# A two-layer decoder on one Trainium2 core: the order of loads, row sums and norms at the start and at the two layer ends

## The reference, cut to what matters

```python
for layer in range(2):
    hn = rmsnorm(h, attn_norm[layer])
    h = h + (even_mixer, odd_mixer)[layer](hn, ...)    # two kinds of attention each, then a projection
    h = h + hierarchical_moe(rmsnorm(h, ffn_norm[layer]), ...)
return rmsnorm(h, final_norm)
```

## Time and profile before

| | |
|---|---|
| median of 3 executions | 1095.43 us (1093.26 to 1098.76) |
| the profiled execution | 1096.88 us, span 1095.0 us |
| mean granted TensorE clock | 0.986 of full |
| PE busy | 1001.8 us (91%) |
| DVE, ACT, POOL busy | 386.8, 233.9, 91.6 us |
| moved by DMA | 276.95 MB, mean 253 GB/s |

### The profile page before, as it was taken

One profiled execution on the slowest core, in us unless ns is written; L12 is line 12 of the kernel. 1 busy time (PEld: TensorE's weight loads), 2 busy tenths in 40 slices (PEclk: granted clock), 3 DMA queues, 4 the chain that ended last, 5 costly groups with the idle time before them and its releaser, 6 DMA issues.

```text
span 1095.0 us, 12899 instructions
## 1 busy us (share of the span) xinstructions
PE 1001.8 (91%) x5140; PEld 575.4 (53%) x5140; DVE 386.8 (35%) x1103; ACT 233.9 (21%) x605; POOL 91.6 (8%) x103
## 2 busy tenths in 40 slices
PE   5999999999998999999788998899999999998866
PEld 3344644455455656666434647536455666665532
DVE  3123621336145323222243316547225333222215
ACT  3122620236011000000022216537202100000002
POOL 2000000000101011211101001000100111111100
PEclk9999999999999999999999999999999999999998
DMA  9522205964336999999999420023624899999996
GB/s 330 215 91 76 77 2 174 210 266 168 120 125 228 407 420 419 420 419 419 421 348 334 165 77 1 11 77 154 237 96 168 325 420 419 421 418 420 416 374 226
DMA packets 63549, 276.95 MB, mean 253 GB/s; under 512 B 12787, under 2 KB 17379, under 8 KB 38906
## 3 DMA queue, kind: packets, MB, share of 16 engines
q1 hardware_dynamic: 53088, 256.95, 60.9%
q0 software_dynamic: 10400, 19.16, 5.0%
HBM read 261.94 MB, written 30.44 MB: 267 GB/s over the span
## 4 chain that ended last, share of the span: by engine, by line
PE 66%; DMA 20%; DVE 5%; SPq 3%; issue 2%; ACT 2%; POOL 1%; POOLq 0%; DVEq 0%; ACTq 0%
PE bank L841 13%; PE bank L931 10%; PE bank L1054 9%; PE bank L853 9%; DMA K<-rows,small 7%; PE bank L872 5%; PE bank L1068 5%; DMA D<-in_moe_w_down 5%; DMA hnT<-in_moe_w_down 3%; PE bank L883 3%; DMA W<-in_moe_w_up 2%; PE bank L899 2%; SPq L449 2%; PE bank L1241 2%; DMA oT<-in_o_w_in 1%
## 5 line engine op out<-in xcount | busy, mean ns | idle before, releaser
L841 PE MATMUL bank<-hnT,W 128*128 128x512 f32 x336 | 145.1, 593 | 0.8 <-ACT hnT L1334 0.8
L1068 PE MATMUL bank<-D,PT 128*64 128x512 f32 x416 | 105.1, 611 | 10.1 <-DMA D<-in_moe_w_down 7.4
L841 PEld LDWEIGHTS bank<-hnT,W 128*128 128x128 f32 x336 | 63.5, 190 | 80.5 <-issue 79.5
L1054 PE MATMUL bank<-W,PT 128*64 128x256 f32 x640 | 78.6, 386 | 13.0 <-DMA W<-in_moe_w_up 6.7
L1759 DVE SCALAR_TENSOR_TENSOR PT<-bank,small,PT 128x256 f32<-128x256 f32 x32 | 15.5, 484 | 210.8 <-PE bank L1054 210.8
L1781 DVE SCALAR_TENSOR_TENSOR K<-K,small,bank 128x512 f32<-128x512 f32 x64 | 47.8, 747 | 86.7 <-PE bank L1068 86.5
L1054 PE MATMUL bank<-W,cst 128*64 128x256 f32 x640 | 77.5, 381 | 0.0
L872 PE MATMUL bank<-K,Q 128*128 128x256 f32 (+3 forms) x256 | 70.4, 417 | 6.1 <-ACT K L1353 3.4
L853 PE MATMUL bank<-W,hnT 128*128 128x512 f32 (+2 forms) x256 | 71.4, 439 | 0.0
L1368 ACT ACTIVATE P<-P,nm 128x256 f32<-128x256 f32 (+3 forms) x128 | 68.3, 535 | 14.6 <-DVE nm L1551 14.1
L1408 ACT ACTIVATE PT<-bank 128x256 f32<-128x256 f32 x32 | 12.3, 384 | 271.9 <-PE bank L1060 271.9
(11 more groups left out here) (245 smaller groups left out, 1364.1 us busy)
## 6 DMA issues: line engine op xcount, KB each, us to landing
D<-in_moe_w_down SPq DMA_DIRECT2D x48, 1024.0 KB, 22.8
W<-in_moe_w_gate SPq DMA_DIRECT2D x40, 1024.0 KB
W<-in_moe_w_up SPq DMA_DIRECT2D x40, 1024.0 KB, 19.6
hnT<-in_moe_w_down SPq DMA_DIRECT2D x12, 1024.0 KB, 17.7
W<-in_e_w_in SPq DMA_DIRECT2D x5, 2048.0 KB
expert_rows<-K SPq DMA_DIRECT2D x2, 4096.0 KB, 34.8
V<-in_moe_w_gate SPq DMA_DIRECT2D x6, 1024.0 KB
Q<-in_moe_w_gate SPq DMA_DIRECT2D x6, 1024.0 KB
```

The source lines that it names most:

```text
L841: last = nc.tensor.matmul(b[:, :], w[:, k, 128 * fb:128 * fb + 128], hnT[:, k, :], start=(k == 0), stop=(k == KD - 1))
L1054: last = nc.tensor.matmul(bank[b][at, 0:256], XT[k // 4][:, k % 4, at], w[:, 256 * k:256 * k + 256], start=(k == 0), stop=(k == KD - 1))
L1068: last = nc.tensor.matmul(bank[5 + half][at, :], hT[:, 128 * c + 64 * a:128 * c + 64 * a + 64], d[:, col:col + 512], start=(c == 0), stop= ...
```

## The change

It has five parts.

1. Start: `gain` for the first norm is loaded by SP as the second transfer, ahead of `cst`, on a semaphore of its own; POOL's load and SP's wait for it go. The transposes of odd chunks use banks 1 and 2, and DVE and ACT copy later in their order.
2. The up weights of experts 30 and 31 come in four half loads, the first halves of both on `s_ulast`; PE waits for each half by itself.
3. Layer 0: the oT weights are issued ahead of all rows, before SP's wait for the scatters.
4. DVE runs `add_row(0)` ahead of `finish(lay, 15)`, and norms chunk 0 (layer 0) before `add_row(1)`. In layer 0, PE transposes chunk 0 after all four late products.
5. Layer 1: PE adds `y_in` by the identity for chunk 3 only (before: chunks 1 and 2); DVE adds chunks 1 and 2.

```diff
-        summed = [(), (1, 2)]
+        first_bank = (3, 1)
+        summed = [(), (3,)]
...
             for c in range(C):
                 sp.dma_start(h[:, c, :], x[0, 128 * c:128 * c + 128, :]).then_inc(s_x[c], 16)
                 if c == 0:
+                    sp.dma_start(gain, attn_norm[0:1, :].partition_broadcast(128).rearrange("a b n -> a (b n)"))\
+                      .then_inc(s_gain0, 16)
                     sp.dma_start(cst[:, 0:C_MASKS], const_table[:, 0:C_MASKS]).then_inc(s_const, 16)
...
-                    load_half(lay, 2 * p, 1)
-                    load_half(lay, 2 * p + 1, 1)
+                    if p < NP - 1:
+                        load_half(lay, 2 * p, 1)
+                        load_half(lay, 2 * p + 1, 1)
+                    else:
+                        for part in range(2):
+                            for e in (2 * p, 2 * p + 1):
+                                up = expert_slot(lay, e)[0][1]
+                                half = slice(DM * part, DM * part + DM)
+                                sp.dma_start(up[:, half], wu_v[lay][e][:, half])\
+                                  .then_inc((s_ulast, ups_landed(lay, p)[0])[part], 16)
...
-            sp.wait_ge(s_gain, 16)
...
             def load_expert_rows(lay):
+                if lay == 0:
+                    sp.wait_ge(s_gu, 11)
+                    load_cols("oT", odd_tile[0], owin_v, 0, 512)
                 for i in range(NB):
                     sp.wait_ge(s_sc[i], 16 * SCATTERS[i] * (lay + 1))
...
                 for c in range(C):
-                    if lay == 0 and c == 3:
-                        load_cols("oT", odd_tile[0], owin_v, 0, 512)
...
-            load_gain(0)
...
-                    if c:
-                        pe.wait_ge((s_ntA, s_ntV)[half], c)
+                    if c >= 2:
+                        pe.wait_ge((s_ntA, s_ntV)[half], c - 1)
...
-                    pe.wait_ge(*ups_landed(lay, p))
-                    product(3, [slot[0][1] for slot in pair], lambda half: None).then_inc(s_gu, 1)
+                    landings = [ups_landed(lay, p)] * 2
+                    if p == NP - 1:
+                        landings[0] = s_ulast, 32 * (lay + 1)
+                    product(3, [slot[0][1] for slot in pair], lambda half: pe.wait_ge(*landings[half])).then_inc(s_gu, 1)
...
-                    if c == 3 and lay == 0:
-                        transpose_second(0)
...
+            transpose_second(0)
             latent_rows(0)
...
                 add_row(0)
+                finish(lay, NP - 1)
                 add_late(0)
                 if lay == 0:
+                    norm_chunk(2, 0)
                     add_row(1)
-                    norm_chunk(2, 0)
                     add_late(1)
...
                 else:
+                    add_row(1)
+                    add_late(1)
                     norm_chunk(4, 0)
-                    add_late(1)
-                    add_row(3)
+                    add_row(2)
+                    add_late(2)
                     norm_chunk(4, 1)
-                    add_late(2)
                     add_late(3)
...
             for c in range(C):
                 norm_chunk(0, c)
-                if c:
-                    norm_out(c - 1)
+                if c >= 2:
+                    norm_out(c - 2)
+            norm_out(C - 2)
             norm_out(C - 1)
...
-            finish(0, NP - 1)
...
-            finish(1, NP - 1)
```

More of the change, by code:

```diff
@@ L324, in trunk @@
         s_dlast = sem("last_down_halves_loaded")
+        s_ulast = sem("last_ups_first_halves_loaded")
         s_half = sem("half_of_first_tile_loaded")
         s_gain = sem("gain_loaded")
+        s_gain0 = sem("first_gain_loaded")
         s_sq = sem("squares_summed")
@@ L805, in transpose_normed @@
                 for half in range(2):
-                    if c:
-                        pe.wait_ge((s_ntA, s_ntV)[half], c)
+                    if c >= 2:
+                        pe.wait_ge((s_ntA, s_ntV)[half], c - 1)
                     for kk in range(4):
                         k = 4 * half + kk
-                        last = nc.tensor.transpose(bank[3 + half][:, 128 * kk:128 * kk + 128],
+                        last = nc.tensor.transpose(bank[first_bank[c % 2] + half][:, 128 * kk:128 * kk + 128],
                                                    hn_row[:, c, 128 * k:128 * k + 128], ident)
@@ L1303, in norm @@
                     mean_root(v, c)
-                    if v == 0 and c >= 2:
-                        norm_out(c - 2)
+                    if v == 0 and c == 2:
+                        norm_out(0)
                     if v == 2 and c == 0:
@@ L1311, in norm @@
                 if v == 0:
-                    norm_out(2)
-                    norm_out(3)
+                    for c in range(1, C):
+                        norm_out(c)
                 if v == 2:
@@ L1334, in norm_out @@
                 nc.scalar.activation(hnT[:, 0:4, 128 * c:128 * c + 128],
-                                     bank[3][:, :].rearrange("p (k t) -> p k t", k=4), ACT.Copy).then_inc(s_ntA, 1)
+                                     bank[first_bank[c % 2]][:, :].rearrange("p (k t) -> p k t", k=4), ACT.Copy)\
+                  .then_inc(s_ntA, 1)
             def norm_out_second(c):
@@ L1510, in norm_chunk @@
                 if c == 0:
-                    dve.wait_ge(s_gain, 16 * (v // 2 + 1))
+                    dve.wait_ge(*((s_gain, 16 * (v // 2)) if v else (s_gain0, 16)))
                 nc.vector.scalar_tensor_tensor(hn_row[:, c, :], h[:, c, :], rstd[:, c:c + 1], gain,
@@ L1517, in norm_out @@
                 nc.vector.tensor_copy(hnT[:, 4:8, 128 * c:128 * c + 128],
-                                      bank[4][:, :].rearrange("p (k t) -> p k t", k=4)).then_inc(s_ntV, 1)
+                                      bank[first_bank[c % 2] + 1][:, :].rearrange("p (k t) -> p k t", k=4)).then_inc(s_ntV, 1)
             def norm_out_second(c):
```

## The result

The changed kernel takes 1104.83 us, the median of five executions (1101.74 to 1105.68). Five executions of the kernel before have the median 1097.33. The ratio is 1.0066, 95% interval [1.0053, 1.0079], so it is slower by some 7.2 us. Forecast were 3.2 us more, and the time is above the end of the range (1102.5). The profiled execution took 1104.83 us with a span of 1102.9 us and a mean granted clock of 0.987. DMA moves the same 276.95 MB, and PE is busy for 997.2 us where it was for 1001.8, so what the kernel is longer by is waiting of PE.

A forecast was written before the change was run, and what follows sets the result against it. PE was taken as the bound, DMA-saturated expert stretches moving with it. Start -1.3, layer 0 +3.2, layer 1 +1.1 and half loads +0.2 gave +3.2 on 1095.4, so 1098.6 us; 8-in-10 range 1091.0 to 1102.5.

The forecast's parts named there:

- R: End of layer 0: landing time of chunk 0's rows, 564.5 before the change, taken as 568.8 after it.
- the term of layer 0: End of layer 0: later end of the first latent product, R - 565.6 = +3.2 us, bounds +1.0 and +4.3.
- even sharing: End of layer 0: the DMA engines share the work evenly, so R is 566.6 and the loss +1.0 us.
- the last engine: End of layer 0: on the engine busy until 562.0, rows pay for all of oT; R 569.9, loss +4.3 us.
- the hole of 555 to 560: End of layer 0: DMA engines only 0.60 busy from 555 to 560, a hole of 2 us that oT fills.
- Start: Kernel start: PE's first long product at 16.9 instead of 18.22, -1.3 us, bounds -1.7 and 0.
- the first norm is not sooner: Rival at the kernel start: constants late, 1.3 us more, total 1099.9 us; chance 0.08.
- Halved ups: Last ups end 1.1 us sooner in layer 0, 3.5 in layer 1, but later waits take it: no gain.
- Layer 1: End of layer 1: new order gives -0.6, a clock drop from PE's idling makes it +1.1 us, bounds -0.6, +1.3.
- the 0.2 charged: Half loads of the last ups: 0.2 us for rows of 4 KB instead of 8 KB, between 0 and 0.5.
- finish is held longer still: Rival, DVE's queue, end of layer 0: R 571.5, term +5.9, total 1101.3, slower by over 0.5%; chance 0.20.
- the first rival: End of layer 0: rows not held up by oT, R stays 564.5, last term -2.8, total 1090.7 us; chance 0.24.

The follow-up runs named there:

- the order alone: The kernel before with add_row(0) put ahead of finish in both layers and nothing else; 1097.38 us, ratio 1.0014 [1.0001, 1.0026].

## Why the prediction was wrong

**The step that failed: R, the landing of chunk 0's rows.** The mechanism stood there, `finish` and every late product behind rows that are behind oT. Its size did not stand: the term of layer 0 was +3.2 and measured +5.6. I had R between even sharing (566.6) and the last engine (569.9), took 568.8 and so gave the hole of 555 to 560 some of its worth. The 566.6 does not even follow from my numbers: the landing of before, oT and the hole give 564.5 + 5.5 - 2.0 = 568.0. The runs deny the hole its worth. The hole is filled (0.60 to 1.02), and the rows still come 7.8 us after the last down half in all three kernels with oT ahead and the halves visible (564.39 to 572.15, 564.26 to 572.04, 564.69 to 572.47), against 3.1 with oT behind (562.29 to 565.38). The difference, 4.7 us here and 5.3 against the 2.5 of before, is nearly the whole 5.4 of oT.

Counted from the first expert product (350.82 instead of 348.89), R is at 221.3 where my last-engine value was at 221.0 and my choice at 219.9; over the five kernels with oT ahead of all rows it is at 221.2 to 223.0. The bytes moved say that the engines did not share evenly. From the start of the execution to R the changed kernel has moved 146.13 MB, the kernel before to its own R (564.5) 142.70. That is 3.43 MB more, and oT is only 2.10 of them; the other four kernels with oT ahead have 146.17 to 146.28, the one with the order alone 142.78. The remaining 1.3 MB stand behind chunk 0's rows in SP's queue, so part of the engines was past these rows while others still had them to move. The Trainium skill (DMA: Bandwidth & Descriptors, section Queues, rings and completion order) has each engine take the descriptors of a ring in order, and completion not follow the order of issue across the engines; the landings and these bytes agree with it, though no trace here shows a single engine. By it alone the term would have been +4.3.

**The clock.** I costed one slow chunk, 1.7 us, for PE's idle time of 7 us. The granted clock stayed low from 570.2 to 580.4, through the first 6.1 us of the late products: 3.0 us more on PE, and the chain took R + 21.2 where I had R + 20.2. With PE kept busy it took R + 18.8, 2.4 less. So the mis-sized term is R by 1.4 us (570.2 on the clock of before's experts, instead of 568.8), and the chain from R by 1.0.

**Start.** Forecast -1.3, measured +0.4 in the profiled execution and -0.5 on the mean of the traces. Gain ahead of the constants cost them 2.6 us and not 1.1: ACT began at 7.70 where I had 6.2, 1.5 later and beyond the 1.3 of my bound. And gain stands ahead of `x` too: with the constants early, the second chunk held ACT to 9.32, and my sum had ACT take it at 7.8 without a wait. The rival "the first norm is not sooner" was right.

**Halved ups.** No gain was forecast and none came (1.0006). The reason was the forecast one in layer 0 only, where the down products wait for their weights (1.15 and 0.39 us). In layer 1 of that kernel nothing waits for the down weights: the second ups (3.68 us) and the downs (5.56) ran slowly, at a granted clock of 0.50 from 1065 to 1074.

**Layer 1.** Forecast +1.1, measured +0.4. The order of part 5 is worth 1.1 us from the late products to the last norm (15.0 to 13.9; 1.0 by itself, where I had 0.6); `finish` behind the rows gives it back with the 1.57 us wait. The clock fell earlier than I had it, in the down products, and the late products ran at full.

**The whole.** 3.2 were forecast and 7.95 found between the two profiled executions: 2.4 of the 4.75 missing are the end of layer 0, 1.7 the start, 1.5 the stretch that no edit touches, and 0.9 less is in layer 1 and the 0.2 charged. The rival that held, "finish is held longer still", had the sign and the place, with R at 571.5 (572.15 measured) and 1101.3 us. Its reason, that chunk 0 also pays for POOL's gain load and the last scatter, is not isolated by any run. On the clock of before's experts R is 570.2, which oT counted whole explains (569.9); in three of the other four kernels with oT ahead it is 571.5 to 571.9, as the rival had it. The rival kept my terms for the chain behind R and for the start, which were off as above, so that its 1101.3 comes near is partly luck. My own sum adds up as written, but for 0.2 us left out of the first rival's 1090.7.

**Left open.** The three traces with oT ahead have the last down half at 213.6 to 215.2 us after the first expert product, the four with it behind at 213.1 to 213.9; whether oT also slows transfers issued before it was not isolated. Nor was why the two edits of layer 0 cost 5.8 us apart and 8.2 together, if they do. One part of it may be layer 1, where DVE waits 3.25 us for chunk 0's rows in their common kernel and 2.52 with the order alone. Whether the halved ups make the loss in layer 0 larger, by letting PE stand still for longer (7.98 us against 4.14), has no run of its own.

## What to carry to other kernels

A hole in the mean DMA share was no room here: the transfer moved ahead of another cost the latter nearly its whole length, counted from the landing of the last byte queued before, so put one ahead only of what nobody waits for. Do not place an add that waits for a late transfer ahead of the step that frees another engine; even undisturbed it cost 1.5 us here, and with a later landing over 3. When a wait of PE is removed, look at the next one behind it and at the clock there; the load split in two brought the late products forward in the two traces where the down products behind it ran at the full clock, and not in the traces where they ran slowly.

## What was unexpected in the hardware

- Around 7.98 us of idling the clock was half for 10.2 us, 6.1 of them with PE at work, three of those lost; eight unused products in that gap kept it at 1.00. It was at half for nine microseconds and more (0.50 from 1065 to 1074) around a wait of only 3.17 us in the kernel with halved ups. A shorter gap went either way: the latent product took 8.80 us after a wait of 2.72, 7.10 after 2.32 in the kernel with halved ups, and 9.05 after 1.49 where a wait of 4.28 stood shortly before. Where no edit stands behind it, such a clock drop is a difference of 1.7 us between executions.
- A transfer of 0.5 MB put ahead of the constants at the start delayed them by 2.2 to 2.6 us, though 0.5 MB take 1.4 us at the 380 GB/s of the earlier trace rows.
- SP needed 2.5 to 2.9 us to issue chunk 0's two sets of rows in the five kernels with oT ahead of them, and 0.85 before (558.47 to 559.32).
